# Turning the softmax reciprocals for a transposed attention output: one transpose of widened rows in place of two matmuls with the identity

## What is computed

```
s = jnp.einsum('bqhd,bkhd->bhqk', qblk, k).astype(jnp.float32) * scale
p = jax.nn.softmax(s, axis=-1).astype(v.dtype)
return jnp.einsum('bhqk,bkhd->bqhd', p, v)
```

## Time and profile before

| | us |
|---|---|
| median of 3 runs | 1138.98 |
| lowest and highest run | 1138.32, 1143.58 |
| span of the profiled execution, first to last instruction | 1138.1 |
| TensorE busy in it | 1042.1 (92%) |
| VectorE busy | 337.7 (30%) |
| ScalarE busy | 256.1 (23%) |
| GpSimd busy | 113.0 (10%) |

### The profile page before, as it was taken

The page is one execution under the profiler, slowest core; times in us unless marked ns, Lnnn a source line. Parts: engine busy times, 40 slices in busy tenths (PEclk is TensorE's granted clock), DMA queues, the critical chain, the costliest instruction groups (busy, mean ns, idle before and its releaser), DMA issues. The chain is left out here.

```text
span 1138.1 us, 16374 instructions
## 1 busy us (share of the span) xinstructions
PE 1042.1 (92%) x6617; PEld 506.9 (45%) x6617; DVE 337.7 (30%) x838; ACT 256.1 (23%) x604; POOL 113.0 (10%) x137
## 2 busy tenths in 40 slices
PE   5899899998999999988699989999989999998967
PEld 3445456654434444333244554666444344433324
DVE  3100465412722222112330026542173222221224
ACT  2110254512211111111221014542131111111132
POOL 4120100001001111110022020000010111111000
PEclk8899999998999999999899999999989999999997
DMA  9941466614899999999994225662298999999981
GB/s 351 384 159 74 158 233 222 222 40 162 322 332 322 401 393 397 398 402 411 385 340 154 84 103 223 223 222 75 100 349 305 353 344 395 401 396 412 410 317 56
DMA packets 70291, 313.84 MB, mean 276 GB/s; under 512 B 7786, under 2 KB 10054, under 8 KB 49984
## 3 DMA queue, kind: packets, MB, share of 16 engines
q1 hardware_dynamic: 61280, 288.54, 66.3%
q0 software_dynamic: 8064, 21.01, 5.3%
q10 hardware_dynamic: 864, 3.15, 0.7%
HBM read 301.32 MB, written 18.58 MB: 281 GB/s over the span
## 5 line engine op out<-in xcount | busy, mean ns | idle before, releaser
L938 PE MATMUL psum<-arena 128*64 128x512 f32 x512 | 236.1, 608 | 18.1 <-DMA arena<-in_w_up 11.6
L941 PE MATMUL psum<-arena 128*64 128x512 f32 x512 | 236.6, 609 | 0.0
L938 PEld LDWEIGHTS psum<-arena 128*64 128x64 f32 x512 | 69.1, 140 | 164.9 <-issue 162.6
L992 PE MATMUL psum<-arena 128*64 128x512 f32 x512 | 120.5, 602 | 3.8 <-ACT arena L1399 2.1
L1775 DVE SCALAR_TENSOR_TENSOR arena<-arena,psum 64x768 f32<-64x768 f32 (+1 forms) x32 | 26.1, 814 | 273.0 <-ACT arena L1393 273.0
L1258 PE MATMUL psum<-arena 128*128 128x384 f32 x256 | 86.3, 492 | 0.0
L1393 ACT ACTIVATE arena<-psum 64x768 f32<-64x768 f32 (+1 forms) x32 | 22.3, 697 | 280.3 <-PE psum L941 280.3
L1113 PE MATMUL psum<-arena 128*128 128x384 f32 x256 | 83.5, 487 | 1.2 <-PE psum L1101 0.6
L941 PEld LDWEIGHTS psum<-arena 128*64 128x64 f32 x512 | 69.1, 140 | 0.0
L1113 PEld LDWEIGHTS psum<-arena 128*128 128x128 f32 x256 | 48.3, 190 | 36.9 <-issue 4.0
L1258 PEld LDWEIGHTS psum<-arena 128*128 128x128 f32 x256 | 47.5, 190 | 32.4 <-issue 0.7
(11 more groups left out here) (273 smaller groups left out, 1245.9 us busy)
## 6 DMA issues: line engine op xcount, KB each, us to landing
arena<-in_w_down SPq DMA_DIRECT2D x64, 1024.0 KB, 16.7
arena<-in_w_gate SPq DMA_DIRECT2D x54, 1024.0 KB, 14.5
arena<-in_w_up SPq DMA_DIRECT2D x54, 1024.0 KB, 17.0
arena<-in_w_ada SPq DMA_DIRECT2D x24, 2048.0 KB, 7.9
arena<-in_w_in SPq DMA_DIRECT2D x6, 2048.0 KB, 17.2
arena<-in_w_gate SPq DMA_DIRECT2D x20, 512.0 KB, 17.5
arena<-in_w_up SPq DMA_DIRECT2D x20, 512.0 KB, 18.5
arena<-in_w_out SPq DMA_DIRECT2D x4, 2048.0 KB, 7.9
```

Of the source, the lines that this page charges most:

```text
L938: ins = nc.tensor.matmul(bank[b][0:MAIN, :], hg[:, k, 0:MAIN], row(wg[half], k), start=(k == 0), stop=(k == KD - 1))
L941: ins = nc.tensor.matmul(bank[b][MAIN:P, :], hg[:, k, 0:MAIN], row(wu[half], k), start=(k == 0), stop=(k == KD - 1))
L992: ins = nc.tensor.matmul(bank[6][MAIN * j:MAIN * j + MAIN, :], hidT[:, c, 0:MAIN], w[half][:, c % 2, 512 * j:512 * j + 512], start=(c == 0 ...
```

## The change

The matmuls with the identity go. VectorE writes the two reciprocals out 64 times each, into 128 columns of a row buffer (`rsum_rows`, two of them in turn, in the memory of `work`, which attention does not use), and TensorE turns those 128 columns with one transpose. TensorE now waits for the new semaphore `rsum_wide`. VectorE waits for its own reciprocal before it copies, and from the third unit on for `probT_ps` of unit u - 2, because that unit's transpose has read the buffer.

```
-                            pe.wait_ge(rsum_ready, UNITS * l + u + 1)
-                            for h in range(2):
-                                r = rsum[:, 2 * (u % 2) + h:2 * (u % 2) + h + 1].to_broadcast([P, HD])
-                                ins = nc.tensor.matmul(bank[4][HD * h:HD * h + HD, n:n + P], r, ident, start=True, stop=True)
+                            pe.wait_ge(rsum_wide, UNITS * l + u + 1)
+                            ins = nc.tensor.transpose(bank[4][:, n:n + P], rsum_rows[:, u % 2, :], ident)
...
                     v.reciprocal(rsum[:, c:c + 2], sums[:, cs:cs + 2]).then_inc(rsum_ready, 1)
+                    dve.wait_ge(rsum_ready, UNITS * l + u + 1)
+                    if u >= 2:
+                        dve.wait_ge(probT_ps, 2 * UNITS * l + 2 * u - 2)
+                    v.tensor_copy(rsum_rows[:, u % 2, :].rearrange("p (h d) -> p h d", h=2),
+                                  rsum[:, c:c + 2].unsqueeze(2).to_broadcast([P, 2, HD])).then_inc(rsum_wide, 1)
```

More of the change, by code:

```diff
@@ L270, in build @@
         cmp = work[:, 0:4 * 48]
+        rsum_rows = tiles(work[:, 0:2 * P], 2)
         group_hot = tiles(take(12), NT)
@@ L308, in build @@
         lora_stat, lora_norm, kr_ready, q_roped, kr_spread = (sem(n) for n in ("lora_stat", "lora_norm", "kr_ready", "q_roped", "kr_spread"))
-        bias_added, rsum_ready = sem("bias_added"), sem("rsum_ready")
+        bias_added, rsum_ready, rsum_wide = sem("bias_added"), sem("rsum_ready"), sem("rsum_wide")
         score_ps, max_ready, exp_ready, probT_ps, probT_act, probT_dve, o_ps, o_ready = (sem(n) for n in (
```

## The result

| | before | after |
|---|---|---|
| median of the first comparison (4 runs each) | 1139.05 us | 1131.38 us |
| lowest and highest run | 1138.32, 1143.58 | 1129.90, 1131.90 |
| ratio, 95% interval | | 0.9926 [0.9906, 0.9946] |
| span of the profiled execution | 1138.1 us | 1129.0 us |
| mean granted clock in it | 0.970 | 0.974 |

A forecast was written before the change was run, and what follows sets the result against it. Attention was taken as bound by TensorE's stream; savings of 2.44 us a layer, 4.9 in both, with VectorE's added work covered, gave 1134.1 us from the median. Own range 1132.3 to 1136.0; 8 in 10: 1131.0 to 1138.8.

The forecast's parts named there:

- An ordinary unit saves 0.11: TensorE from last transpose of probabilities to first value: 0.47 us before, 0.36 after, in 16 units a layer.
- Fold units save 0.34: Units 11 and 23 of each layer: last transpose to 128-wide fold takes 0.22 us instead of 0.56.
- Units 0, 3, 6, 9, 21 and 22 save nothing: Six of 24 units a layer give savings back waiting: the first four for VectorE's bank 5 copy, 21 and 22 for ScalarE's.
- Attention's sum: 16 units saving 0.11 and two saving 0.34: 1.76 + 0.68 = 2.44 us a layer, 4.9 in both.
- The widening copy: VectorE's added SBUF-to-SBUF copy, 128 elements per partition: 0.28 us taken, bounds 0.17 and 0.34; stream grows 15 us in all.
- It lasts to the end: Behind attention, experts' weight DMAs move forward with TensorE, so no loss is counted from the 4.9 us.
- a median of a few runs another ±1: Allowance in the total's range for run spread, beside ±1.2 us for swallowed units and step costs.
- half-clock stretches that differ by more than 3 us between the profiles: Sign that the prediction is wrong: time at half clock differing by more than 3 us between both profiles.
- A: Rival, chance 0.18: swallowed units count too, 6.2 us gained (1132.8), or one half-clock stretch less, 3.5 us (1130.7).
- C: Rival, chance 0.08: slower by the clock, two more half-clock stretches cost 6.9 us and give 1141.0.
- B: Rival, chance 0.17: nearly nothing gained, widened rows late in most units or experts' DMA waits growing; 1138.
- D: Rival, chance 0.02: a transpose step costs 0.055 us, not 0.11, saving 2.0 us more; 1132.1.

The follow-up runs named there:

- the last kernel: Kernel with bank 5's copy moved and reciprocals early in units 4, 7, 10, now copying conditioning rows in unit 22, not 21: attention 74.82 and 74.83 us, total median 1128.46.

## Why the prediction was right in mechanism and wrong in size
- **TensorE bounds attention.** Right. VectorE's work could grow by 5 and by 8 us without any effect.
- **An ordinary unit saves 0.11.** Right: 0.103 to 0.112 in the 16 units named, in both layers. The four removed instructions and the added one came to a saving of one step, as worked out.
- **Fold units save 0.34.** Each saved 0.46. The prediction put the stretch behind the fold's start at nothing ("What follows the fold is as before"), and that is the term of attention's sum that failed: the fold's second matmul starts 0.03 behind the first in place of 0.135, because the first weight load is hidden now. It is worth 0.1 a place.
- **Units 0, 3, 6, 9, 21 and 22 save nothing.** Right. The first five change by 0.006 at most. Unit 21 gives its saving back to VectorE's copy of bank 5, for which unit 22 waits 0.20 in place of 0.10, and not to ScalarE as I had it. Unit 22 is 0.10 shorter up to the first transpose of unit 23 (its widened rows came in time by 0.1, where I had them late by 0.1), and gives it back there: the weight load for the second half of `turned(23)` waits 0.39 for ScalarE's copy, where the earlier trace rows have 0.28.

```profile
218.51 0.31 PEld L1209 LDWEIGHTS psum<-arena 128*128 128x128 f32 x3 [0.39 <-ACT arena L1472]
```

- **Attention's sum.** 16 ordinary units of 0.108, two fold units of 0.457 and -0.01 for 22 with 23 make 2.63 a layer, instead of 2.44. So of the 0.4 us that both attentions gave beyond the forecast, all is the fold.
- **The widening copy.** 0.227 us, within the bounds of 0.17 and 0.34, below the value taken. The Trainium skill, "VectorE: DVE Perf Modes", section "Mode 2×_2P — use both read ports for one tensor", has such a copy move two elements a cycle; the estimate from it was 0.22, and the trace agrees with it rather than with the row from PSUM, here with a source that repeats each element. That the mode is the reason isn't shown: no run varies the size of this copy. VectorE's stream grew by 10.1 us of busy time; the prediction's 15 us would have been a fifth of VectorE's free time in the attentions, not a third.
- **It lasts to the end.** Right as far as it can be told: 5.3 in attention, 4.7 ± 1.1 in the total. In the profile after, TensorE waits for the experts' weights 1.1 us longer than in the earlier trace rows, 12.7 in place of 11.6:

```profile
L939 PE MATMUL psum<-arena 128*64 128x512 f32 x512 | 236.4, 609 | 19.2 <-DMA arena<-in_w_up 12.7
```

- **The step that failed** for the total is the last term, "a median of a few runs another ±1". The forecast was 1134.1 with its own range from 1132.3, and the comparison gave 1131.38. The runs show a standard deviation of 2.5 us for one run, with medians of 12 runs of the same kernel at 1133.57 and 1134.69 and of four at 1131.38. From that, a median of four runs is uncertain by some ±3 us (an estimate), and a difference of two such medians by ±4. Of the 2.8 us between 4.9 and 7.7, attention gave 0.4; the rest was luck of the first runs. The prediction named its own sign for this, half-clock stretches that differ by more than 3 us between the profiles: they do, by 4.8 (0.030 × 1138.1 = 34.1 lost before, 0.026 × 1129.0 = 29.4 after). For such stretches it had a rival on either side (A and C), with a price of the right size, but no spread for them around the forecast itself.
- **Rivals.** A's first half (swallowed units count too) fell; its clock half is what the first comparison showed, as chance. B fell: no unit waited for widened rows (the new transpose starts 0.11 behind the last one in all 48 units), and the experts' waits took at most 1.1 us. C fell, since the change was faster on every occasion. D fell; a transpose took a step of 0.11.

## What to carry to other kernels
Price a matmul on a full TensorE stream by the distance of starts, not by its duration or by counting instructions: pairs in different column groups share a step, a change of width adds 0.09 to a step and 0.05 to the next, and a float32 transpose is one step where a matmul is two. Then go through the units one by one and ask what the next wait hangs on; six of 24 units gave their saving back here, and that list could be worked out from the waits in the trace of the kernel before. And when an effect of half a per cent is to be judged, measure the stage that was changed, which repeats within 0.02 us, beside the total, whose single runs spread over 8.

## What the runs showed of the hardware that was not expected
- A stream of small matmuls (eight columns) goes by its weight loads, one in 0.11 us. Behind a transpose the first load is hidden and the second matmul starts after 0.03 us; behind a change of width it is in the open and the second starts after 0.135. A change of width isn't the only thing that does this: in the last kernel, where the fold of unit 23 started late behind a transpose of its own width, the second matmul started after 0.10.
- Executions of one and the same kernel grant between 0.967 and 0.977 of full clock on one core with nothing else running, and the total follows: some 0.8 us for each 0.001, by a straight line fitted through the runs with one height for each kernel. Which stretches fall to 1.2 GHz changes between executions, ahead of the first attention and behind each of the two; within an attention the granted clock was 1.00 in every profile.
- Moving a wait on VectorE by one unit cost 2.1 us a layer: VectorE waited for the exps up to 1.3 us at a time, what stood behind in its stream was late with it, and TensorE's units 1, 4, 7 and 22 grew by 0.5 to 0.8 us.
